# The up projection in seven block products over half of its depth, with the samples' rows held stationary

## The reference

```python
def hybrid_layer(x, ...):
    ...
    x = x + merged @ w_out
    f = rmsnorm(x, norm2_w) @ w_up          # (tokens, 1024) @ (1024, 4096)
    x = x + jnp.square(jax.nn.relu(f)) @ w_down   # (tokens, 4096) @ (4096, 1024)
    return x, new_conv, k, v
...
y_prompt = rmsnorm(xp, norm_f_w)
y_sample = rmsnorm(xs, norm_f_w)
```

## Time and profile before

| what | us |
| --- | --- |
| median of three runs | 1613.08 |
| the profiled execution, as a run | 1613.12 |
| its span in the trace | 1611.4 |
| TensorE busy | 1600.1 |
| VectorE busy | 1057.3 |
| ScalarE busy | 533.8 |
| GpSimd busy | 725.1 |

### The profile page before, as it was taken

One profiled execution on the slowest core, in us unless ns is written; L12 is line 12 of the kernel. 1 busy time (PEld: TensorE's weight loads), 2 busy tenths in 40 slices (PEclk: granted clock), 3 DMA queues, 4 the chain that ended last, 5 costly groups with the idle time before them and its releaser, 6 DMA issues.

```text
span 1611.4 us, 25421 instructions
## 1 busy us (share of the span) xinstructions
PE 1600.1 (99%) x9776; PEld 1482.7 (92%) x9776; DVE 1057.3 (66%) x1408; ACT 533.8 (33%) x1047; POOL 725.1 (45%) x597
## 2 busy tenths in 40 slices
PE   9999999999999999999999999999999999999998
PEld 8999999999998888999988989999999999999996
DVE  7685877859712221356433588777778888877777
ACT  6655665556522221432134411111111111111124
POOL 5212121121212111223587486666666776666653
PEclk9999999999999999999999999999999999999999
DMA  4201112011184767372354111110111111111012
GB/s 165 68 27 55 54 40 69 27 41 55 41 281 149 234 222 231 117 244 96 129 186 144 58 53 52 53 42 16 49 53 53 52 53 53 53 53 51 18 51 111
DMA packets 133491, 144.99 MB, mean 90 GB/s; under 512 B 7839, under 2 KB 98619, under 8 KB 133372
## 3 DMA queue, kind: packets, MB, share of 16 engines
q1 hardware_dynamic: 133226, 143.34, 27.8%
q10 hardware_dynamic: 146, 0.04, 0.0%
HBM read 124.37 MB, written 18.98 MB: 89 GB/s over the span
## 4 chain that ended last, share of the span: by engine, by line
PE 87%; DVE 8%; ACT 3%; issue 1%; DVEq 0%; ACTq 0%
PE ps L1307 51%; PE ps L1641 6%; PE ps L1642 6%; PE ps L1643 6%; DVE sp L2140 2%; PE ps L1598 2%; PE ps L1603 2%; PE ps L1601 2%; PE ps L1501 2%; DVE zc L2132 1%; PE ps L1457 1%; PE ps L1467 1%; PE ps L1545 1%; PE ps L1513 1%; ACT sp L1815 1%
## 5 line engine op out<-in xcount | busy, mean ns | idle before, releaser
L1307 PE MATMUL ps<-xh,wh 128*128 128x352 f32 (+1 forms) x956 | 322.3, 337 | 0.9 <-DVE xl L2113 0.7
L1307 PE MATMUL ps<-xh,wl 128*128 128x352 f32 (+1 forms) x956 | 312.5, 327 | 0.0
L1307 PE MATMUL ps<-xl,wh 128*128 128x352 f32 (+1 forms) x956 | 312.2, 327 | 0.0
L2269 DVE TENSOR_TENSOR x<-ps,x 128x1024 f32<-128x1024 f32 x210 | 257.1, 1225 | 42.9 <-PE ps L1643 24.5
L1150 POOL CAST wh<-raw 128x1024 fp32r<-128x1024 f32 x48 | 50.4, 1050 | 477.6 <-issue 213.2
L1307 PE MATMUL ps<-yh,wh 128*128 128x384 f32 (+1 forms) x768 | 250.5, 326 | 0.0
L1307 PE MATMUL ps<-yh,wl 128*128 128x384 f32 (+1 forms) x768 | 250.5, 326 | 0.0
L1307 PE MATMUL ps<-yl,wh 128*128 128x384 f32 (+1 forms) x768 | 250.2, 326 | 0.0
L1939 ACT ACTIVATE hf<-hf 128x384 f32<-128x384 f32 (+1 forms) x96 | 48.6, 508 | 554.9 <-DVE hf L2322 554.9
L1307 PEld LDWEIGHTS ps<-xh,wh 128*128 128x128 f32 x956 | 179.8, 188 | 17.2 <-issue 15.5
L1307 PEld LDWEIGHTS ps<-xl,wh 128*128 128x128 f32 x956 | 180.0, 188 | 0.7
(11 more groups left out here) (214 smaller groups left out, 3148.9 us busy)
## 6 DMA issues: line engine op xcount, KB each, us to landing
raw<-in_w_in SPq DMA_DIRECT2D x80, 256.0 KB, 3.3
cache<-in_cache_k SPq DMA_DIRECT2D x64, 256.0 KB, 3.8
cache<-in_cache_v SPq DMA_DIRECT2D x64, 256.0 KB, 3.6
raw<-in_w_up SPq DMA_DIRECT2D x64, 256.0 KB, 5.2
raw_d<-in_w_down SPq DMA_DIRECT2D x30, 512.0 KB, 4.1
raw<-in_w_out SPq DMA_DIRECT2D x48, 256.0 KB, 2.9
gates<-gst SPq DMA_DIRECT2D x16, 544.0 KB, 5.9
gb<-gates SPq DMA_DIRECT2D x16, 544.0 KB, 5.4
```

The costliest lines, as they stand in the source:

```text
L1307: ins = mm(out, lhs[:, k * P:(k + 1) * P], rhs[:, x], start=(first and a == 0 and m == 0), stop=(last and a == n - 1 and m == 2))
L2269: V_.tensor_tensor(x, src, x, ALU.add).then_inc(step_free, 1)
```

## The change

The first two up tiles are computed as before, but with the depth tiles in another order (4 to 7 first) and in more pieces, since `yh` and `yl` are now cut into tiles of their own for each block. The other 30 up tiles are done in pairs, 2n and 2n+1 in one group of entries "mix":

- Over depth tiles 4 to 7 the product is plain: 4 tiles, 2 weight tiles, 2 token halves of 512, 3 matmuls each, 48 in all.
- Over depth tiles 0 to 3 it is done in seven products of blocks (2 depth tiles, one weight tile, 512 tokens; 6 matmuls each, 42 in all). Their token operands are the blocks of `y` and four differences of them, made once ("twist" and "twist_low": VectorE, ScalarE, VectorE). Their weight operands are the blocks of `w_up` and four twists of them, made for every pair.
- The samples' 64 columns no longer move behind the prompt's. `y_few` holds their high and low columns side by side as a stationary operand; 256 columns of weights, high and low, move past it (16 matmuls). ScalarE copies the 128 rows of the result to `few_rows`, and two small float32 matmuls against `both` (two identities, one above the other) add high and low rows and turn them ("mix" 8).

"mix" 0 to 7 are the seven products and the plain work, laid so that partial results are used twice: products 0, 2 and 4 build up in one bank, and ScalarE copies a bank into `hf` between them ("keep"). VectorE adds the second part from PSUM onto that copy ("join"), and ScalarE does the positive part and the square in place. Before, VectorE took the positive part and ScalarE the square.

The up weights now come as six operands of 512 columns a pair ("u", 0 to 5) and share the ring of 5 slots with the eight of the down product, so that 14 operands a cycle pass through it. ScalarE casts u0 to u3 ("u_cast"), behind the product stage; GpSimd makes their low parts, and all of u4 and u5. Two of the four `sum` buffers are gone: sums 2 and 3 are written over sum 0 once ScalarE has cast what stood in it. In the diff the first "join" is VectorE's share, the second ScalarE's.

```diff
+        MIX = [("x", 0, None), ("y", 1, (0, 0)), ("z", 3, None), ("x", 2, None), ("z", 5, (0, 1)), ("x", 4, None), ("w", 6, (1, 0)),
+               ("x", None, (1, 1))]
...
         for n in range(1, N_TWIN):
-            tail += [("sum", n - 1, k) for k in range(4)]
-            todo = list(PREP)
-            for m in range(6):
-                e = 2 * n + m // 3, m % 3
-                tail += [("up", *e), ("relu", *e)]
-                for _ in range(BESIDE_UP[m]):
-                    tail.append(("prep", n - 1, todo.pop(0)))
+            m = n - 1
+            if n == 1:
+                tail += [("u_cast", n, x) for x in range(4)]
+            tail += [("sum", m, 0), ("sum", m, 1), ("mix", n, 0), ("keep", n, 0), ("prep", m, 0), ("prep", m, "few0"), ("prep", m, "few1"),
+                     ("mix", n, 1), ("few_move", n), ("mix", n, 2), ("keep", n, 2), ("mix", n, 3), ("keep", n, 3), ("join", n, 1),
+                     ("prep", m, 1), ("prep", m, 6), ("mix", n, 4), ("mix", n, 8), ("mix", n, 5), ("keep", n, 5), ("prep", m, 3),
+                     ("prep", m, 4), ("join", n, 4), ("join", n, 8), ("sum", m, 2), ("prep", m, 2), ("sum", m, 3), ("mix", n, 6),
+                     ("join", n, 6), ("prep", m, 5), ("mix", n, 7), ("join", n, 7)]
...
             tail += [("prod", n - 1, p) for p in range(1, N_WAY)]
+            if n < LAST_TWIN:
+                tail += [("u_cast", n + 1, x) for x in range(3)]
             tail.append(("few", n - 1, 1))
+            if n < LAST_TWIN:
+                tail.append(("u_cast", n + 1, 3))
...
         def prod_bank_read(n, p, q):
             if p == 0 and q == 0:
-                return read_no["up", 2 * n + 3, 1]
+                return max(read_no["mix", n + 1, m] for m in (6, 8))
...
+        RING = []
+        for n in range(1, N_TWIN):
+            RING += [("u", n, x) for x in range(len(U_LAST))]
+            RING += [("d", n - 1, k) for k in range(N_OP)]
...
+            def up_op(n, x):
+                ...
+                if x < 4:
+                    slot_free(of)
+                    split_op(of, raw_u[:, U_KT[x] * 2 * P:(U_KT[x] + 2) * 2 * P])
+                elif x == 4:
+                    twist(s1, a21, a22, ALU.add)
+                    twist(s2, s1, a11, ALU.subtract)
+                    slot_free(of)
+                    split_op(of, tw[0][:, :])
...
             for n in CYCLES:
-                for k in range(N_SOON):
-                    down_op(n, k)
-                if 2 * n + 4 < 2 * N_TWIN:
-                    tail_tile(N_OUT + 2 * n + 4)
-                for k in range(N_SOON, N_OP):
+                for x in range(len(U_LAST)):
+                    up_op(n + 1, x)
+                for k in range(N_OP):
...
                     down_op(n, k)
-                if 2 * n + 5 < 2 * N_TWIN:
-                    tail_tile(N_OUT + 2 * n + 5)
...
+                elif e[0] == "join":
+                    v.wait_ge(step_done, done_no["mix", n, m])
+                    if m < 8:
+                        ...
+                        V_.tensor_tensor(x, bank(MIX_BANK[MIX[m][0]]), x, ALU.add).then_inc(step_free, 1)
...
+                elif e[0] == "join":
+                    act.wait_ge(step_free, read_no["mix", n, m])
+                    ...
+                            A(x, x, ACT.Relu).then_inc(relu_made, 1)
+                            act.wait_ge(relu_made, 4 * (n - 1) + RELU_NO[m])
+                        A(x, x, ACT.Square).then_inc(hf_made, 1)
```

More of the change, by code:

```diff
@@ L93, in hybrid_layer @@
         ident = place("ident", [P, P], F32)
+        at_consts = cursor[0]
         ones = place("ones", [P, P], F32)
@@ L193, in hybrid_layer @@
         low_rows = place("low_rows", [P, D], F32, at + 8 * D)
-        assert at + 20 * D <= ry + 8 * WIDE
+        assert at + 20 * D <= ry + 6 * KQ * ROW + 4 * KT * SEQ
         cursor[0] = r2
@@ L801, in hybrid_layer @@
                 is_read(("up", *e[1:]))
+            elif e[0] == "mix":
+                done += 1
+                done_no[e] = tile_end["up", 2 * e[1] + 1] = done
+            elif e[0] == "join":
+                is_read(("mix", *e[1:]))
             elif e[0] == "prod":
@@ L1232, in tail_tile, with twist, slot_free, split_op @@
                 g.tensor_tensor(low[:, :], raw[n % 3][:, :], f32(high[:, :]), ALU.subtract).then_inc(w_split, 1)
+            turns = [0]
+            def twist(out, one, other, op):
+                g.tensor_tensor(out, one, other, op).then_inc(t_made, 1)
+                turns[0] += 1
+                pool.wait_ge(t_made, turns[0])
+            def slot_free(of):
+                pool.wait_ge(step_done, slot_after[of])
+                if of == TOP_FIRST:
+                    pool.wait_ge(twist_lo, 4)
+                apart(pool)
+            def split_op(of, src):
+                high, low = w_hi_at[slot_of[of]][:, :], w_lo_at[slot_of[of]][:, :]
+                kind, n, x = RING[of]
+                if kind == "u" and x < 4:
+                    pool.wait_ge(u_hi, 4 * (n - 1) + x + 1)
+                else:
+                    g.tensor_copy(high, src).then_inc(d_hi, 1)
+                    pool.wait_ge(d_hi, of + 1 - 4 * n if kind == "u" else of + 1 - 4 * (n + 1))
+                g.tensor_tensor(low, src, f32(high), ALU.subtract).then_inc(d_lo, 1)
+                pool.wait_ge(d_lo, of + 1)
+            def up_op(n, x):
+                rows_ = blocks(raw_u, 2 * P)
+                a11, a12, a21, a22 = (rows_[:, KQ * j:KQ * j + KQ, i * P:i * P + P] for i in range(2) for j in range(2))
+                s1, s2, s4, s3 = (blocks(tw[t])[:, KQ * h:KQ * h + KQ, :] for t in range(2) for h in range(2))
+                of = ring_no["u", n, x]
+                if x == 0:
+                    pool.wait_ge(u_in, 32 * n)
+                if x < 4:
[6 more added lines that the diff above has]
+                    split_op(of, tw[0][:, :])
+                else:
+                    twist(s3, a11, a21, ALU.subtract)
+                    twist(s4, a12, s2, ALU.subtract)
+                    slot_free(of)
+                    split_op(of, tw[1][:, :])
             def down_op(n, k):
@@ L1689, in _ @@
                     pe.wait_ge(w_split, base + n + 1)
-                    pe.wait_ge(step_free, up_bank_read(j, c))
-                    for half in range(2):
-                        if j < 2:
-                            pe.wait_ge(y_lo, 6 * [p for p in range(3) if PASSES[p][0][0] == 3 * c][0] + 5 + half)
-                        ins = product(bank(up_bank(j, c), 0, z - a), wh[n % 2], wl[n % 2], range(4 * half, 4 * half + 4), yh, yl, (a, z),
-                                      first=half == 0, last=half == 1)
+                    pe.wait_ge(step_free, step_no["up", j, c] + 1)
@@ new lines, in _ @@
+                    pe.wait_ge(y_lo, 6 * [p for p in range(3) if PASSES[p][0][0] == 3 * c][0] + 6)
+                    order_ = [*range(KT // 2, KT), *range(KT // 2)]
+                    for f in order_:
+                        pieces = y_pieces(f, a, z)
+                        for piece in pieces:
+                            out = bank(up_bank(j, c), piece[0] - a, piece[1] - a)
+                            for m, (w, part) in enumerate(((wh, 0), (wh, 1), (wl, 0))):
+                                ins = mm(out, w[n % 2][:, f * P:(f + 1) * P], y_at(f, part, *piece), start=(f == order_[0] and m == 0 and piece == pieces[0]),
+                                         stop=(f == order_[-1] and m == 2), skip_group_check=True)
```

319 lines of the change are left out of this document (237 added, 82 removed).

## The result

The changed kernel takes 1700.13 us (median of four runs, 1699.1 to 1700.94) against 1613.08: a ratio of 1.0539, with a 95% interval of 1.0521 to 1.0557. It is slower, as forecast, but by 87 us and not by 55: the forecast was 1668, the range 1622 to 1698, and the time lies 2 us outside it.

What follows compares the result with a forecast made beforehand. TensorE was taken as the bound. Per cycle -1.2 + 3.2 + 1.2 = +3.2 us, +48 over 15 cycles; first up tiles +1.5, first cycle +5.5: +55 on 1613.1 gives 1668 us, range 1622 to 1698.

Steps and rivals of the forecast that it cites:

- Where the wait is and who ends it: Ahead of the product stage's first down product, TensorE waits for VectorE's join of "mix" 6: 3.2 us in each cycle.
- The undisturbed rest: Stall ahead of the first down product if GpSimd did not disturb VectorE: 0.3 us a cycle.
- The second wait: Second down product waits for bank 7 to come back from the samples' addition: 1.2 us in each cycle.
- The clock: TensorE's clock is granted in full, 2.4 GHz, throughout; no cost in the sum.
- Rival D: After a 3 us stall, first down product and samples' matmuls run at 1.2 GHz: 2.4 us a cycle, 1704; chance 0.07.
- The saving: Up stage of each cycle: fewer matmuls take 1.2 us less of TensorE's time, 18 us over 15 cycles.
- The first two up tiles: Ahead of the cycles, stretches cut into more pieces, many of 64 columns, cost 1.5 us more in all.
- The first cycle: ScalarE's late fourth "twist" cast delays the weight casts and GpSimd's low part: 5.5 us once, from 3 to 8.
- The further 1 us for u1 to u4: In the first cycle, 1 us added because these up weight operands come one by one.
- C: GpSimd becomes the chain, making TensorE wait 1 to 2 us more a cycle at "mix" 2: 1683 to 1698; chance 0.13.
- A: TensorE never waits in the cycles, so the kernel gets faster: -11 us, 1602; chance 0.08.

## Why the prediction was right in its sign and too low

**Where the wait is and who ends it: right.** Each cycle has the wait of "prod" 0 for the join of "mix" 6, 3.57 us where 3.2 were forecast. The chain came as written: low parts 3 and 4, join, the small ones, sum 2, low part 2 behind ScalarE, sum 3, join. Its price came from the rows where VectorE and GpSimd exclude each other, and the run with GpSimd's work thinned out confirmed it: 2.8 us of the wait are GpSimd's, where 2.9 were forecast. The undisturbed rest was 0.77 and not 0.3. Part of the closeness is luck: the forecast gave every such instruction the same 0.65 us, and the thinned run took 1.8 off low parts 3 and 4 together, 0.61 off low part 2, 0.41 off "sum" 3 and 0.25 off "sum" 2.

**The second wait: somewhat too large, and wrong in its count.** 0.85 us in three cycles (forecast 1.2), and in all 15 once the clock was kept up. Where the clock fell, "prod" 0 took longer and hid it.

**The clock: the step that failed.** The sum had the clock at nothing. The forecast wrote "No row shows it idle for more than 1.1 us" and then took 2.4 GHz as its likeliest case, with 0.07 for a fall. But the forecast's own wait of 3.2 us was outside of all that the trace of before had shown, so that its rows could not speak for a full clock behind it. The trace of before even holds a fall, at its very end, which the forecast did not look at:

```profile
1605.00:1611.40 6.40, 0.00 (x0) 0.00 (x0) 3.26 (x7) 1.67 (x4) 0.00 (x0) 0.72 0.61 246
```

TensorE's last matmul had ended at 1604.6; the granted clock of this stretch is 0.72 because it is full at first and half from 1607.9 on. In the changed kernel the fall came in 12 of 15 cycles. Rival D had priced it at 2.4 us net a cycle for "prod" 0 and the samples' matmuls at half rate, 1704 in all; measured are 10.5 us in 14 cycles, 0.75 a cycle and also net of the second wait, since a stretch lies partly over the wait itself and costs nothing there. The two changes of the sum that D needed were right in kind (more for the clock, less for the second wait) and three times too large. D comes closest to the measured 1700 all the same, because other terms were too low. With the 2.8 us of the first stage the clock cost some 13 us; without them the time would have been about 1687, inside the range.
The Trainium skill ("TensorE: Matmul & The Clock Gate", section "What's actually happening"), which the forecast had cited beside D, has the slow clock as the default that activity lifts; the trace agrees, and the run that filled the wait with 15 matmuls shows it best, at a clock of 0.997 where the changed kernel has 0.981.

**The saving: mis-sized.** Forecast -1.2 us a cycle; measured 44.14 - 44.70 = -0.56 where nobody waits long. (The first of the 14 cycles of before took 45.35 us and the others 44.63, so that against a plain cycle the saving is 0.49.) One up stage of the changed kernel is 23.27 us against 23.72, and not 22.5. TensorE in it: the last of the samples' matmuls, and the two small float32 ones (four instructions in the record).

```profile
1128.57 0.28 PE L1866 MATMUL ps<-d_lo,y_few 128*128 128x256 f32 x1
1129.04 0.47 PE L1828 MATMUL ps<-yh,d_hi 128*128 128x512 f32 x1 [0.19 <-POOL d_lo L1344]
...
1135.96 0.55 PE L1872 MATMUL ps<-both,few_rows 128*128 128x64 f32 x4
1136.32 0.48 PE L1828 MATMUL ps<-yh,d_hi 128*128 128x512 f32 x1
1136.64 0.39 PE L1828 MATMUL ps<-yl,d_hi 128*128 128x512 f32 x1
```

The 16 of 256 columns start 0.12 apart, as forecast (1.9 us in all). The small ones cost 0.36 and one of 0.32 behind them (0.09 over the pitch) where 0.2 was taken. "mix" 2 loses 0.35 to GpSimd each time (0.47 from the start of the last row of 256 columns to the next start, less 0.12). These make 0.6 of the 0.75 that is missing; the rest is a few hundredths here and there, which I did not resolve. Behind a long wait there is 0.24 more a cycle: 44.14 + 3.57 + 0.85 = 48.56 where 48.8 was measured; the first two starts behind the wait are 0.31 and 0.24 apart already ahead of the clock fall.

**The first two up tiles: mis-sized by 3.8 us.** Forecast +1.5, from a line through 320, 384 and 512 columns that was drawn on down to 64, with an upper bound of 3.3 + 1.1; measured +5.3 (32.08 - 26.75), above the bound. TensorE there:

```profile
905.14 0.36 PE L1819 MATMUL ps<-yh_aside,wh 128*128 128x256 f32 x1
905.35 0.28 PE L1819 MATMUL ps<-yl_aside,wh 128*128 128x256 f32 x1
905.47 0.28 PE L1819 MATMUL ps<-yh_aside,wl 128*128 128x256 f32 x1
905.58 0.30 PE L1819 MATMUL ps<-y_few,wh 128*128 128x64 f32 x2
905.72 0.28 PE L1819 MATMUL ps<-y_few,wl 128*128 128x64 f32 x1
905.83 0.36 PE L1819 MATMUL ps<-yh,wh 128*128 128x256 f32 x1
```

The three pieces of 64 columns take 0.25 us from 905.58 to 905.83, and the first piece of 256 behind them 0.20 to 0.21 in place of 0.12, in each depth tile. Per depth tile it is 0.25 + 0.44 = 0.69 us, where one stretch of 320 columns took 3 x 0.146 = 0.44; over 16 depth tiles that is 4.0 us. The other 1.3 are the 8 depth tiles in which a stretch of 384 columns is cut into 128 and 256: these take 0.69 us where they took 3 x 0.174 = 0.52. No run tested other pieces.
The Trainium skill ("TensorE: Matmul & The Clock Gate", section "Wait — 56ns, not 53.3ns?") has a floor of 25 ns between starts for small matmuls. In these fp32r rows the first two of 64 columns start about 0.03 us apart, near that floor, but the next two distances are 0.11 us each, and the next one of 256 is late besides; the mean of the three, 83 ns, is well above the page's floor.

**The first cycle: the wait right, the clock missing.** The chain came as written: ScalarE's fourth "twist" cast (917.17 to 918.23), three squares, the cast of u0, then GpSimd's low part, which ended at 921.26. It was forecast at 4.5 us and cost 4.34. The further 1 us for u1 to u4 did not come, and the clock fall behind it, 2.8 us, was not in the sum. That the two together, 7.1, lie within 3 to 8 is luck in part. With the casts moved forward the fall went and 3.2 us of wait stayed, for GpSimd's low parts: ScalarE's order is the cause of the long single wait, but not of all that is lost there.

**C and A.** GpSimd did not become the chain in the cycles: it costs 0.35 us a cycle at "mix" 2. The half twists took 1.07 and 0.74 where C asked for 1.2; with the casts put back on GpSimd, C's wait begins to appear (half a microsecond more a cycle). A, TensorE never waiting, had 1602 as its time. The run nearest to it gives 1619, because the products' saving was half of what was taken and the first and the last cycle cost 13 us of their own.

**A slip in the chances.** The forecast gives 1640 to 1688 for waits of 2 to 5.5 us a cycle; by its own sum 2 us a cycle make 1613 + 12 + 7 = 1632. Nothing hangs on it.

**The sum again, as measured**: a cycle -0.56 + 3.57 + 0.85 + 0.24 + 0.75 for the clock = +4.85, times 14 = 67.9; before the first "prod" 0 +16.0; behind the last +3.1; together 87.0. The forecast's cycle was +3.2. Of the 32 us between forecast and measurement, 23 lie in the 14 cycles (0.64 a cycle from the saving, 0.37 from the first wait, 0.75 from the clock, 0.24 from slower starts, -0.35 from the second wait), and the rest in the first and the last one.

## What to carry to other kernels

When a forecast holds a wait longer than any that the trace has, the granted clock behind it is unknown too, and belongs in the sum with a bound on both sides, less what of the slow stretch lies over the wait. An engine that stands idle ahead of an entry in a strictly ordered list, and is late two entries on, wants its list turned round: here two entries put ahead of one wait were worth 62 us, and 78 with the order changed further. A change that saves half a microsecond a cycle must be charged with its first and its last cycle before it is built: those 13 us are more than 14 cycles gave.
